# Query products in high and low parts, rotation on VectorE, and one product for the decay rows

## The chip, the cores and the metric

One core of a Trainium2 chip runs the whole kernel in one launch. The engines that matter here: TensorE (PE) multiplies matrices into PSUM banks, VectorE (DVE) and ScalarE (ACT) read those banks and prepare operands, SyncE (SP) issues most transfers, GpSimd (POOL) the rest. Each engine runs its own list of instructions in order and waits on semaphores for the others. The metric is the time of one execution on the device in microseconds (us); lower is better.

## The reference, cut to what matters

The kernel computes one step of a decoder layer for a prompt of 512 tokens and 8 requests of 4 sample tokens (544 columns). The part that is touched is the mixer:

```python
proj = h @ lw['w_in']                      # 44 units of 128 columns
cq = rmsnorm(cq, lw['norm_q_lat'])         # 256 latent features
q = (cq @ lw['w_uq']).reshape(B, T, H_B, NOPE_DIM + ROPE_DIM)
q_rope = rope(q[..., NOPE_DIM:], pos)      # [x1*cos - x2*sin, x2*cos + x1*sin]
kr = rope(kr[:, :, None, :], pos)[:, :, 0, :]
q_lat = jnp.einsum('bthd,chd->bthc', q_nope, lw['w_uk'])
s = jnp.einsum('bthc,bsc->bhts', q_lat, ckv) + jnp.einsum('bthr,bsr->bhts', q_rope, krope)
# softmax of SM_SCALE * s, times ckv, for 8 heads; mLSTM, 4 heads, with decays
D = b[..., :, None] - b[..., None, :] + ic[..., None, :]
```

## The kernel before, in words

Activations lie transposed: 128 features on partitions, tokens as columns. The big products split each fp32 operand in a high part (rounded to the fp32r type) and a low part (the rest), and add three fp32r products: high x high, high x low, low x high. ACT writes the high part (`w_hi`, L1602), DVE the low one (`w_lo`, L2275). One unit of the input projection is 48 such products of 272 columns on PE (L1156). The 41 units from the fourth on are the filler of the whole mixer: on every engine a generator `in_feed` holds its share of the units, and `dense(n)` lets n steps of it pass, a step being one product on PE. What stands between the calls of `dense` is the attention or the mLSTM. The order is thus written out by hand, for each engine by itself.

At the end of each half of a unit DVE evicts it from PSUM (`evict`, L2750). A gate's unit goes to `gt`, ACT writes its tanh to `sg` (`tanh_gate`, L1933), DVE turns that into the gate in `sq` (`gate`, L2765, L2766, L2769), and SP spills `sq` to DRAM (L687). `gt`, `sg` and `sq` have two slots each.

The heads of the attention come in four pairs. For a pair, `query` (L1226) makes three banks of 512 columns, two with the part without rotation (one per head) and one with the rotary part of both heads, each by two fp32 products of `wp` and `cq`; ACT copies them to `qn` and `qrx` (the tile is named accq). `latent_queries` multiplies `qrx` by a permutation matrix (L1233), so that each half of the rotary features stands where the other was, and makes the latent queries (L1235). `rotate` on DVE (L2896 to L2902) multiplies the permuted bank by sin and `qrx` by cos, and adds the two, once in place and twice with the 64-row parts exchanged. `two_scores` (L1257, L1261) waits for it. The keys of the prompt are rotated once in the same way (L1187, L2828 to L2832). The queries of pair 0 stand ahead of the heads; those of pair p+1 stand in the heads of pair p, one bank in each of three places and the latent queries in the fourth.

A head: ACT copies the scores (`take`), DVE masks them and finds the maximum (`highest`), ACT takes exp (`expo`, L2051), DVE divides (`normalise`, L2919), PE transposes (`turn`), ACT copies back (`turned`), PE multiplies by the values. The sample tokens run beside it, through `sample_highest`, `sample_exp`, `sample_turned` (L2082) and `sample_values` (L1329), with the new rows at the start of pairs 0 and 2 (`sample_new`: pnn L2934, prob L2066, L1313).

The mLSTM begins each of its four heads with one fp32 product of 4 rows that spreads the decay row of the head over 128 partitions (L1398); ACT copies it to `nmb`.

## Time and profile before

| | us |
|---|---|
| median of 3 runs | 1341.14 (1340.37 to 1341.49) |
| the profiled execution | 1342.6 |
| its span, first to last instruction | 1340.9 |
| PE busy | 1309.8 (98%) |
| DVE busy | 946.7 (71%) |
| ACT busy | 590.3 (44%) |
| POOL busy | 144.6 (11%) |

The clock that PE was granted is full speed over nearly the whole span (mean 0.998). Busy times of PE overlap, since its products are pipelined: how long one keeps the engine is read from the start of one record to the start of the next, not from its duration. An fp32 product is two records, an fp32r product one. The heads of the attention lie between 478 and 725 us, the mLSTM after that.

### The profile page before, as it was taken

To read this page: it belongs to the slowest core of one execution; us is meant where nothing else is said; L and a number is where in the kernel's file an instruction comes from. 1 tells how busy PE (TensorE), PEld (TensorE's weight loads), DVE (VectorE), ACT (ScalarE), POOL (GpSimd) and SP (SyncE) were. 2 spreads that over 40 slices of the span, in tenths; PEclk is the share of its full clock that TensorE was granted. 3 is DMA by queue.
4 is the path that set the end of the run, shared out by engine and by line. 5 is a ranking of instruction groups with operands and counts; after the bars stand their busy time and mean duration, and the time that the engine had idled before them with its cause. 6 is when DMAs were issued, how large, how long until landed. Compare 5 with 4: busy or idle time off the path is not lost.

```text
span 1340.9 us, 30484 instructions
## 1 busy us (share of the span) xinstructions
PE 1309.8 (98%) x11641; PEld 1229.3 (92%) x11641; DVE 946.7 (71%) x1833; ACT 590.3 (44%) x1127; POOL 144.6 (11%) x275
## 2 busy tenths in 40 slices
PE   9999999999999999999999999999899999999997
PEld 8999999999989968888888888889899999999996
DVE  5999889984497544544444665575889989989556
ACT  5455555652354334433344233233544555555323
POOL 0000000000004105555552000000000000000000
PEclk9999999999999999999999999999999999999999
DMA  4232223322246627777777313414152322233322
GB/s 170 87 124 98 95 95 124 119 88 87 83 183 210 217 79 222 239 217 225 216 226 246 131 64 128 152 48 173 68 184 93 106 95 95 95 106 113 107 87 100
DMA packets 86234, 180.85 MB, mean 135 GB/s; under 512 B 12681, under 2 KB 47498, under 8 KB 84042
## 3 DMA queue, kind: packets, MB, share of 16 engines
q1 hardware_dynamic: 77898, 162.12, 36.1%
q0 software_dynamic: 8192, 16.79, 4.5%
q8 instruction: 93, 1.52, 0.5%
q14 instruction: 51, 0.42, 0.1%
HBM read 162.29 MB, written 16.57 MB: 133 GB/s over the span
## 4 chain that ended last, share of the span: by engine, by line
PE 84%; DVE 8%; DMA 3%; ACT 2%; issue 2%; SPq 0%; DVEq 0%; ACTq 0%
PE acc L1071 20%; PE acc L1156 18%; PE acc L993 12%; PE acc L844 6%; PE bank_a L1071 6%; PE acc L1017 4%; PE acc L905 2%; PE bank_a L1226 2%; PE bank_a L1257 2%; PE acc L1275 1%; PE acc L1297 1%; DMA w_raw<-in_w_gu 1%; PE acc L1329 1%; PE bank_a L1048 1%; PE acc L1301 1%
## 5 line engine op out<-in xcount | busy, mean ns | idle before, releaser
L1071 PE MATMUL acc<-x_forms,pair_w 128*128 128x272 f32 x1728 | 273.2, 289 | 0.0
L1071 PEld LDWEIGHTS acc<-x_forms,pair_w 128*128 128x128 f32 x1728 | 244.4, 188 | 0.0
L1156 PE MATMUL acc<-x_hi,w_hi 128*128 128x272 f32 x656 | 200.2, 305 | 0.0
L1156 PE MATMUL acc<-x_hi,w_lo 128*128 128x272 f32 x656 | 192.2, 293 | 0.0
L1156 PE MATMUL acc<-x_lo,w_hi 128*128 128x272 f32 x656 | 191.9, 292 | 0.0
L2275 DVE TENSOR_TENSOR w_lo<-w_raw,w_hi 128x1024 fp32r<-128x1024 f32 (+1 forms) x92 | 108.3, 1177 | 100.6 <-ACT w_hi L1602 100.3
L482 POOL DMA_DIRECT2D pg<-in_lat x256 | 137.4, 537 | 199.9 <-issue 134.5
L1602 ACT ACTIVATE w_hi<-w_raw 128x1024 fp32r<-128x1024 f32 (+1 forms) x92 | 93.0, 1018 | 90.8 <-PE acc L1156 38.9
L1156 PEld LDWEIGHTS acc<-x_hi,w_hi 128*128 128x128 f32 x656 | 123.8, 189 | 9.6 <-issue 8.1
L1156 PEld LDWEIGHTS acc<-x_lo,w_hi 128*128 128x128 f32 x656 | 123.9, 189 | 5.2 <-issue 4.7
L1156 PEld LDWEIGHTS acc<-x_hi,w_lo 128*128 128x128 f32 x656 | 123.7, 189 | 3.7 <-issue 3.6
L1071 PE MATMUL acc<-x_r,pair_w 128*128 128x272 f32 x384 | 110.7, 288 | 0.0
L2380 DVE TENSOR_TENSOR pair_w<-w_pair,pair_w 128x512 fp32r<-128x512 f32 x128 | 88.3, 690 | 22.8 <-ACT pair_w L1703 19.5
L993 PE MATMUL acc<-h_hi,w_hi 128*128 128x272 f32 x448 | 97.3, 288 | 0.4 <-DVE w_lo L2275 0.4
L993 PE MATMUL acc<-h_hi,w_lo 128*128 128x272 f32 x448 | 96.8, 288 | 0.0
L993 PE MATMUL acc<-h_lo,w_hi 128*128 128x272 f32 x448 | 96.7, 287 | 0.0
L1703 ACT ACTIVATE pair_w<-w_pair 128x512 fp32r<-128x512 f32 x128 | 80.2, 628 | 34.8 <-PE acc L1071 23.2
L1703 ACT ACTIVATE pair_w<-pair_s 128x512 fp32r<-128x512 f32 x96 | 60.3, 632 | 72.6 <-DVE pair_s L2411 32.4
L1071 PE MATMUL bank_a<-x_forms,pair_w 128*128 128x272 f32 x576 | 80.4, 289 | 0.0
L1071 PEld LDWEIGHTS bank_a<-x_forms,pair_w 128*128 128x128 f32 x576 | 75.5, 188 | 0.0
L1071 PEld LDWEIGHTS acc<-x_r,pair_w 128*128 128x128 f32 x384 | 72.4, 189 | 0.0
L993 PEld LDWEIGHTS acc<-h_hi,w_hi 128*128 128x128 f32 x448 | 71.6, 188 | 0.8 <-issue 0.8
(442 smaller groups left out, 2819.6 us busy)
## 6 DMA issues: line engine op xcount, KB each, us to landing
w_pair<-in_w_gu SPq DMA_DIRECT2D x68, 512.0 KB, 4.3
pg<-in_key_t SPq DMA_DIRECT2D x256, 96.0 KB, 2.5
w_raw<-in_w_in SPq DMA_DIRECT2D x44, 512.0 KB, 4.7
pg<-in_lat POOLq DMA_DIRECT2D x256, 64.0 KB, 2.8
w_raw<-in_w_dn SPq DMA_DIRECT2D x32, 448.0 KB, 3.3
w_raw<-in_w_gu SPq DMA_DIRECT2D x20, 512.0 KB, 3.3
block_raw<-in_w_dn SPq DMA_DIRECT2D x32, 256.0 KB, 3.6
g_mid<-sq SPq DMA_DIRECT2D x17, 272.0 KB, 3.0
```

Of the source, the lines that this page charges most:

```text
L482: eng.dma_start(pg[c % 2][:, q, j, PAGE + ROPE:PGW], one(lat, page_of(eng, c, q, j)))\
L844: ins = nc.tensor.matmul(acc[pair][:, a, 0:HT], w[:, slot, n * P:(n + 1) * P], v[:, k, a * HT:(a + 1) * HT], start=first and n == 0 and te ...
L905: ins = nc.tensor.matmul(acc[pair_of[j]][:, a, 0:HT], w, v[:, k, HALF[a]], start=k == 0 and term == 0, stop=k == KD - 1 and term == 2)
L993: ins = nc.tensor.matmul(acc[u // 2 % 2][:, a, 0:HT], w[:, u % 2, n * P:(n + 1) * P], v[:, k, HALF[a]], start=start and n == 0 and term == ...
L1017: ins = nc.tensor.matmul(bank_of[n], w[:, k * P:(k + 1) * P], v[:, k, :], start=start and k == 0 and term == 0, stop=k == KD // 2 - 1 and ...
L1071: ins = nc.tensor.matmul(bank, w[:, k * P:(k + 1) * P], v[:, k, :], start=start and k == 0 and term == 0, stop=k == KD // 2 - 1 and term == 2,
L1156: ins = nc.tensor.matmul(acc[0][:, a, 0:HT], w[:, i % 2, k * P:(k + 1) * P], v[:, k, a * HT:(a + 1) * HT], start=k == 0 and term == 0, sto ...
L1226: ins = nc.tensor.matmul(b[:], wp[:, k * 384 + m * P:k * 384 + (m + 1) * P], cq[:, k, 0:SEQ], start=k == 0, stop=k == 1)
L1602: nc.scalar.activation(whi[:, slot, 0:tiles * P], raw[:, slot, 0:tiles * P], ACT.Copy)\
L1703: nc.scalar.activation(pair_weight_hi(s, n), pair_form(s, n), ACT.Copy).then_inc(pair_hi, 1)
L2275: nc.vector.tensor_tensor(wlo[:, slot, 0:tiles * P], raw[:, slot, 0:tiles * P], f32(whi[:, slot, 0:tiles * P]), ALU.subtract).then_inc(w_s ...
L2380: nc.vector.tensor_tensor(lo, pair_form(s, n), f32(hi), ALU.subtract).then_inc(pair_split, 1)
```

## The change

Four things change.
- The prompt's query products take `cq` and `wp` in high and low parts: six fp32r products for a bank in place of two fp32 ones. ACT makes the high parts, DVE the low ones: of `cq` once, of `wp` for each pair.
- The permutation products of the prompt queries and of the keys are gone. DVE multiplies by sin in pieces of 32 partitions that read one half and write the other (four for the queries, two for the keys), and subtracts instead of adds.
- The decay product reads `rows_hl` and `sel_hl`, of 36 rows: the high parts in rows 0 to 3 and the low parts in rows 32 to 35, zeros between; it is one fp32r product in place of an fp32 one. Both operands are prepared in head 7 of the attention.
- The tanh is written in place, and the gates are made in `gt` and spilled from it; an eviction into a slot of `gt` waits until that slot's last content is staged or spilled (`gate_staged`, `gate_out`). The space of `sg` and `sq` takes the high parts.

```diff
@@ -112,6 +112,10 @@
...
+def in_gt(i):
+    return IN_KIND[i] not in ("q", "k") or i in SPILL_AT
...
@@ -1183,9 +1193,6 @@
...
             pe.wait_ge(d_read, 4)
-            for a in range(2):
-                nc.tensor.matmul(bank_v(f"kr{a}")[0:ROPE, 0:HT], perm[0:ROPE, 0:ROPE],
-                                 kraw[0:ROPE, a * HT:(a + 1) * HT], start=True, stop=True).then_inc(v_ready, 1)
...
@@ -1220,17 +1227,19 @@
             def query(p, m):
-                pe.wait_ge(pair_landed[0], 16 * (3 + p))
+                pe.wait_ge(wp_split, p + 1)
+                pe.wait_ge(cq_split, 1)
...
                 for k in range(2):
-                    ins = nc.tensor.matmul(b[:], wp[:, k * 384 + m * P:k * 384 + (m + 1) * P], cq[:, k, 0:SEQ],
-                                           start=k == 0, stop=k == 1)
+                    at_ = slice(k * 384 + m * P, k * 384 + (m + 1) * P)
+                    for term, (w, v) in enumerate(((wphi, cqhi), (wphi, cqlo), (wplo, cqhi))):
+                        ins = nc.tensor.matmul(b[:], w[:, at_], v[:, k, 0:SEQ],
+                                               start=k == 0 and term == 0, stop=k == 1 and term == 2)
...
             def latent_queries(p):
                 pe.wait_ge(a_read, A.taken(f"q{p}2"))
-                nc.tensor.matmul(bank_v(f"rot{p}")[:], perm, qrx[:, 0:SEQ], start=True, stop=True).then_inc(v_ready, 1)
...
@@ -1395,7 +1404,8 @@
...
                     pe.wait_ge(head0_landed, 16)
-                nc.tensor.matmul(bank_a(f"bm{h}")[:, 0:SEQ], sel[:, h, :], rows2[0:4, 0:SEQ],
+                pe.wait_ge(hl_split, 1)
+                nc.tensor.matmul(bank_a(f"bm{h}")[:, 0:SEQ], sel_hl[:, h, :], rows_hl[:],
...
@@ -1926,11 +1936,7 @@
             def tanh_gate(i):
                 act.wait_ge(d_read, 2 * i + 2)
-                before = [n for n in TANH_AT if n < i and n % 2 == i % 2]
-                if before:
-                    n = before[-1]
-                    act.wait_ge(gate_staged, STAGED_AT[n + 1 if IN_KIND[n] == "o" else n] + 1)
-                nc.scalar.activation(sg[:, i % 2, :], gt[:, i % 2, :], ACT.Tanh, scale=0.5).then_inc(tanh_done, 1)
+                nc.scalar.activation(gt[:, i % 2, :], gt[:, i % 2, :], ACT.Tanh, scale=0.5).then_inc(tanh_done, 1)
...
@@ -1983,6 +1989,8 @@
...
             nc.scalar.activation(ckvtok[0:NS, NT, :], A.bank("cts")[0:NS, 0:P], ACT.Copy).then_inc(a_read, 1)
+            act.wait_ge(cq_ready, 2)
+            nc.scalar.activation(cqhi[:, :, 0:SEQ], cq[:, :, 0:SEQ], ACT.Copy).then_inc(cq_hi, 1)
...
@@ -2012,6 +2020,15 @@
...
+            def split_pair(p):
...
+                act.wait_ge(pair_landed[0], 16 * (3 + p))
+                if p:
+                    act.wait_ge(a_ready, A.filled(f"q{p - 1}2"))
+                nc.scalar.activation(wphi[:], wp[:, 0:768], ACT.Copy).then_inc(wp_hi, 1)
...
+            split_pair(0)
...
@@ -2107,6 +2124,13 @@
...
                     expo(h, 3)
+                    if h == HB - 1:
+                        act.wait_ge(hl_clear, 1)
+                        nc.scalar.activation(sel_hl[0:4, :, :], sel, ACT.Copy)
+                        nc.scalar.activation(sel_hl[32:36, :, :], sel, ACT.Copy)
+                        nc.scalar.activation(rows_hl[0:4, :], rows2[0:4, 0:SEQ], ACT.Copy).then_inc(hl_high, 1)
+                    if h % 2 == 0 and p + 1 < HB // 2:
+                        split_pair(p + 1)
...
@@ -2726,13 +2750,13 @@
...
                     dve.wait_ge(d_half, i + 1)
-                    before = [n for n in range(4, i) if n % 2 == i % 2 and (n in TANH_AT or turned_here(n))]
-                    if i in SPILL_AT and i not in STAGED_AT:
-                        dve.wait_ge(gate_out[SPILL_AT[i] % 2], 16 * (SPILL_AT[i] // 2))
-                    elif before and (i in TANH_AT or turned_here(i)):
+                    before = [n for n in range(4, i) if n % 2 == i % 2 and in_gt(n)]
+                    if before and in_gt(i):
                         n = before[-1]
-                        if n in TANH_AT:
-                            dve.wait_ge(tanh_done, TANH_AT[n] + 1)
+                        if n in SPILL_AT:
+                            dve.wait_ge(gate_out[SPILL_AT[n] % 2], 16 * (SPILL_AT[n] // 2 + 1))
+                        elif n in TANH_AT:
+                            dve.wait_ge(gate_staged, STAGED_AT[n + 1 if IN_KIND[n] == "o" else n] + 1)
...
@@ -2744,29 +2768,24 @@
...
                 out = (ckvraw[:, h_] if kind == "ckv" else cq[:, int(kind[2]), h_] if kind in ("cq0", "cq1") else
-                       sq[:, SPILL_AT[i] % 2, h_] if i in SPILL_AT and i not in STAGED_AT else
-                       qk[:, head % 2, 0, h_] if kind == "q" else qk[:, head % 2, 1, h_] if kind == "k" else
-                       gt[:, i % 2, h_])
+                       gt[:, i % 2, h_] if in_gt(i) else qk[:, head % 2, 0 if kind == "q" else 1, h_])
...
             def gate(i):
...
                 if i in SPILL_AT:
-                    g = SPILL_AT[i]
-                    if g >= 2:
-                        dve.wait_ge(gate_out[g % 2], 16 * (g // 2))
-                    out = sq[:, g % 2, :]
+                    out = gt[:, i % 2, :]
...
@@ -2822,14 +2841,12 @@
...
             dve.wait_ge(c_landed, 32)
-            for a in range(2):
-                h_ = slice(a * HT, (a + 1) * HT)
-                dve.wait_ge(v_ready, V.filled(f"kr{a}"))
-                nc.vector.tensor_tensor(tmp[0:ROPE, h_], V.bank(f"kr{a}")[0:ROPE, 0:HT], sin[0:ROPE, h_], ALU.mult)\
-                    .then_inc(v_read, 1)
-                link(nc.vector.tensor_tensor(krT[0:ROPE, h_], kraw[0:ROPE, h_], cos[0:ROPE, h_], ALU.mult))
-                dve.wait_ge(v_read, V.taken(f"kr{a}"))
-                nc.vector.tensor_tensor(krT[0:ROPE, h_], krT[0:ROPE, h_], tmp[0:ROPE, h_], ALU.add).then_inc(kr_half, 1)
+            dve.wait_ge(d_read, 4)
+            for b in range(2):
+                mine, other = slice(b * ROPE // 2, (b + 1) * ROPE // 2), slice((1 - b) * ROPE // 2, (2 - b) * ROPE // 2)
+                nc.vector.tensor_tensor(tmp[other, :], kraw[mine, :], sin[mine, :], ALU.mult)
+            link(nc.vector.tensor_tensor(krT[0:ROPE, :], kraw[0:ROPE, :], cos[0:ROPE, :], ALU.mult))
+            nc.vector.tensor_tensor(krT[0:ROPE, :], krT[0:ROPE, :], tmp[0:ROPE, :], ALU.subtract).then_inc(kr_half, 2)
...
@@ -2883,23 +2900,35 @@
...
                                     ALU.subtract).then_inc(row_sums, 1)
+            dve.wait_ge(cq_hi, 1)
+            dve.wait_ge(a_ready, A.filled(f"qs{HB // 2 - 1}"))
+            nc.vector.tensor_tensor(cqlo[:, :, 0:SEQ], cq[:, :, 0:SEQ], f32(cqhi[:, :, 0:SEQ]), ALU.subtract)\
+                .then_inc(cq_split, 1)
...
+            def split_pair(p):
...
+                dve.wait_ge(wp_hi, p + 1)
+                nc.vector.tensor_tensor(wplo[:], wp[:, 0:768], f32(wphi[:]), ALU.subtract).then_inc(wp_split, 1)
...
+            split_pair(0)
...
             def rotate(p):
-                dve.wait_ge(v_ready, V.filled(f"rot{p}"))
-                nc.vector.tensor_tensor(tmp[:, 0:SEQ], V.bank(f"rot{p}")[:], sin[:, 0:SEQ], ALU.mult).then_inc(v_read, 1)
+                dve.wait_ge(a_read, A.taken(f"q{p}2"))
+                for b in range(4):
+                    mine, other = slice(32 * b, 32 * b + 32), slice(32 * (b ^ 1), 32 * (b ^ 1) + 32)
+                    nc.vector.tensor_tensor(tmp[other, 0:SEQ], qrx[mine, 0:SEQ], sin[mine, 0:SEQ], ALU.mult)
                 link(nc.vector.tensor_tensor(qr[:, 0:SEQ], qrx[:, 0:SEQ], cos[:, 0:SEQ], ALU.mult))
-                dve.wait_ge(v_read, V.taken(f"rot{p}"))
                 low, high = slice(0, ROPE), slice(ROPE, P)
-                nc.vector.tensor_tensor(qr_turned[high, :], qr[low, 0:SEQ], tmp[low, 0:SEQ], ALU.add)
-                link(nc.vector.tensor_tensor(qr_turned[low, :], qr[high, 0:SEQ], tmp[high, 0:SEQ], ALU.add))
-                nc.vector.tensor_tensor(qr[:, 0:SEQ], qr[:, 0:SEQ], tmp[:, 0:SEQ], ALU.add).then_inc(qr_ready, 1)
+                nc.vector.tensor_tensor(qr_turned[high, :], qr[low, 0:SEQ], tmp[low, 0:SEQ], ALU.subtract)
+                link(nc.vector.tensor_tensor(qr_turned[low, :], qr[high, 0:SEQ], tmp[high, 0:SEQ], ALU.subtract))
+                nc.vector.tensor_tensor(qr[:, 0:SEQ], qr[:, 0:SEQ], tmp[:, 0:SEQ], ALU.subtract).then_inc(qr_ready, 1)
...
@@ -2990,10 +3019,16 @@
...
                     sample_highest(m0)
+                    if h == HB - 1:
+                        dve.wait_ge(a_ready, A.filled(f"q{HB // 2 - 1}2"))
+                        nc.vector.memset(f32(rows_hl[:]), 0.0)
+                        nc.vector.memset(f32(sel_hl[:]), 0.0).then_inc(hl_clear, 1)
...
                     normalise(h, 1)
+                    if h % 2 == 0 and p + 1 < HB // 2:
+                        split_pair(p + 1)
...
@@ -3002,6 +3037,10 @@
...
                     take_output(h)
+                    if h == HB - 1:
+                        dve.wait_ge(hl_high, 1)
+                        nc.vector.tensor_tensor(rows_hl[32:36, :], rows2[0:4, 0:SEQ], f32(rows_hl[0:4, :]), ALU.subtract)\
+                            .then_inc(hl_split, 1)
```

On DVE, the end of head 1 and the rotation of pair 1, before. The name rt is the tile of `qr`, accq that of `qrx`, acc the PSUM bank with the permuted rows:

```order
L2924 COPY olat<-acc 128x512 [waits v_ready]
L2750 TENSOR_TENSOR gt<-acc,rpre 128x272 [waits w_used]
L2275 TENSOR_TENSOR w_lo<-w_raw,w_hi 128x1024 [waits w_hi]
L2896 TENSOR_TENSOR tmp<-acc,consts 128x512 [waits v_ready]
L2897 TENSOR_TENSOR rt<-accq,consts 128x512
L2900 TENSOR_TENSOR qr_turned<-rt,tmp 64x512 [waits v_read,vchain]
L2901 TENSOR_TENSOR qr_turned<-rt,tmp 64x512
L2902 TENSOR_TENSOR rt<-rt,tmp 128x512 [waits vchain]
L2765 TENSOR_SCALAR sg<-sg 128x544 [waits gate_out1,tanh_done]
```

The same place in the changed kernel:

```order
L2953 COPY olat<-acc 128x512 [waits v_ready]
L2772 TENSOR_TENSOR gt<-acc,rpre 128x272 [waits w_used]
L2299 TENSOR_TENSOR w_lo<-w_raw,w_hi 128x1024 [waits w_hi]
L2926 TENSOR_TENSOR tmp<-accq,consts 32x512 [waits a_read]
L2926 TENSOR_TENSOR tmp<-accq,consts 32x512 x3
L2927 TENSOR_TENSOR rt<-accq,consts 128x512
L2929 TENSOR_TENSOR qr_turned<-rt,tmp 64x512 [waits vchain]
L2930 TENSOR_TENSOR qr_turned<-rt,tmp 64x512
L2931 TENSOR_TENSOR rt<-rt,tmp 128x512 [waits vchain]
L2784 TENSOR_SCALAR gt<-gt 128x544 [waits tanh_done]
```

One product from PSUM has become four of 32 partitions from SBUF; the wait is now for ACT's read of the query bank instead of PE's product, and the place behind the w_lo split is the same.

On DVE, head 2 around the second normalise (`pr`) and the eviction behind it, before:

```order
L2918 RECIPROCAL sst<-sst 128x1 [waits ex_ready]
L2919 TENSOR_SCALAR pr<-pr,sst 128x256 [waits vchain]
L2750 TENSOR_TENSOR gt<-acc,rpre 128x272 [waits tanh_done,d_half]
L2918 RECIPROCAL sst<-sst 128x1 [waits ex_ready]
L2919 TENSOR_SCALAR pr<-pr,sst 128x384 [waits vchain]
```

The same place now:

```order
L2947 RECIPROCAL sst<-sst 128x1 [waits ex_ready]
L2948 TENSOR_SCALAR pr<-pr,sst 128x256 [waits vchain]
L2916 TENSOR_TENSOR wp_lo<-wp,wp_hi 128x768 [waits wp_hi]
L2772 TENSOR_TENSOR gt<-acc,rpre 128x272 [waits gate_staged,d_half]
L2947 RECIPROCAL sst<-sst 128x1 [waits ex_ready]
```

The low half of `wp` stands between them and waits for ACT. On ACT, in the changed kernel, the last exp of head 2 is followed by:

```order
L2068 ACTIVATE pr,sst<-pr,sst 128x384 [waits mx_ready]
L2068 ACTIVATE pr,sst<-pr,sst 128x512 [waits mx_ready]
L2029 ACTIVATE wp_hi<-wp 128x768 [waits a_ready,pair_landed0]
L2099 ACTIVATE probT<-acc 128x512 [waits o_ready,turn_ready]
```

Before, the copy to probT followed the exp at once. PE's list of this head now waits for wp_split ahead of the query products.

## Rows read from the trace of the kernel before

**Rows 1.** The page, busy time, share of the span and instructions of an engine.
```profile
PE 1309.8 (98%) x11641; PEld 1229.3 (92%) x11641; DVE 946.7 (71%) x1833; ACT 590.3 (44%) x1127; POOL 144.6 (11%) x275
```

**Rows 2.** Busy time by stretches, the attention stretch: us, then each engine's busy us.
```profile
478.00:725.00 247.00, 245.18 (x3347) 201.21 (x3345) 122.22 (x325) 101.44 (x244) 120.39 (x228) 1.00 0.70 209
```

**Rows 3.** Waits of PE, 395 to 880 us: total us, times, longest.
```profile
PE acc L1418 <- DVE pt L3034: 1.5, 4, 0.4
...
```

**Rows 4.** Timeline of PE: start us, us, engine, line, operation, tiles, shapes, count.
```profile
468.84 0.29 PE L1156 MATMUL acc<-x_lo,w_hi 128*128 128x272 f32 x1
...
469.97 0.29 PE L1156 MATMUL acc<-x_lo,w_hi 128*128 128x272 f32 x1
...
472.48 5.31 PE L1226 MATMUL bank_a<-cq,wp 128*128 128x512 f32 x12
...
725.14 1.12 PE L1398 MATMUL bank_a<-rpost,consts 4*128 4x512 f32 x2
726.11 0.30 PE L1401 MATMUL bank_a<-rpost,consts 4*128 4x32 f32 x2
```

**Rows 5.** Timeline, rotation of pair 0 (bracketed: idle before, what ended it).
```profile
479.40 1.23 DVE L2275 TENSOR_TENSOR w_lo<-w_raw,w_hi 128x1024 fp32r<-128x1024 f32 x1 [6.28 <-ACT w_hi L1602]
...
480.54 0.69 DVE L2896 TENSOR_TENSOR tmp<-acc,consts 128x512 f32<-128x512 f32 x1
...
483.89 0.18 DVE L2934 TENSOR_TENSOR pnn<-acc,consts 128x32 f32<-128x32 f32 x1
...
484.99 0.28 PE L1313 MATMUL acc<-consts,prob 128*32 128x128 f32 x1 [0.94 <-ACT prob L2066]
```

**Rows 6.** Timeline, rotation of pair 1 and the scores that follow on PE.
```profile
543.57 0.68 DVE L2896 TENSOR_TENSOR tmp<-acc,consts 128x512 f32<-128x512 f32 x1
544.17 0.68 DVE L2897 TENSOR_TENSOR rt<-accq,consts 128x512 f32<-128x512 f32 x1
...
544.88 0.69 DVE L2900 TENSOR_TENSOR qr_turned<-rt,tmp 64x512 f32<-64x512 f32 x1
545.58 0.69 DVE L2901 TENSOR_TENSOR qr_turned<-rt,tmp 64x512 f32<-64x512 f32 x1
546.31 0.69 DVE L2902 TENSOR_TENSOR rt<-rt,tmp 128x512 f32<-128x512 f32 x1
...
547.39 0.92 PE L1257 MATMUL bank_a<-ckvT,ql 128*128 128x128 f32 x4
```

**Rows 7.** Timeline, before the rotations of pairs 2 and 3 and after them.
```profile
600.31 0.43 DVE L2750 TENSOR_TENSOR gt<-acc,rpre 128x272 f32<-128x272 f32 x1
...
606.57 0.35 DVE L2959 SCALAR_TENSOR_TENSOR o_acc<-o_acc,sm_al,acc 128x128 f32<-128x128 f32 x1 [0.81 <-PE acc L1329]
...
664.43 0.43 DVE L2750 TENSOR_TENSOR sq<-acc,rpre 128x272 f32<-128x272 f32 x1
...
671.46 0.71 PE L1257 MATMUL bank_a<-ckvT,ql 128*128 128x128 f32 x3
```

**Rows 8.** Timeline, head 2: second normalise, last exp, next query on PE.
```profile
555.35 0.35 DVE L2919 TENSOR_SCALAR pr<-pr,sst 128x256 f32<-128x256 f32 x1
...
555.91 0.19 ACT L2051 ACTIVATION_READ_ACCUMULATOR pr<-pr,sst 128x1 f32 x1
...
557.66 1.88 PE L1226 MATMUL bank_a<-cq,wp 128*128 128x512 f32 x4
```

**Rows 9.** Timeline, head 7: the copy to probT and the products that read it.
```profile
707.68 0.58 ACT L2082 ACTIVATE probT<-acc 128x512 f32<-128x512 f32 x1
...
709.60 1.08 PE L1329 MATMUL acc<-pg,probT 128*32 128x128 f32 x32
```

**Rows 10.** The page's DMA issues (count, KB, us to landing); two timeline rows.
```profile
g_mid<-sq SPq DMA_DIRECT2D x17, 272.0 KB, 3.0
...
465.90 0.35 SPq L687 DMA_DIRECT2D g_mid<-sq  x1
...
469.68 0.44 DVE L2750 TENSOR_TENSOR gt<-acc,rpre 128x272 f32<-128x272 f32 x1 [0.81 <-PE acc L1156]
```

More of the change, by code:

```diff
@@ L199, in layer @@
         sq = put("sq", [P, 2, T])
+        wphi, cqhi = at("wp_hi", [P, 768], SG_AT, F32R), at("cq_hi", [P, 2, T], SQ_AT, F32R)
         w_pair0 = at("w_pair0", [P, 2, 2 * QW], SQ_AT)
@@ L248, in layer @@
         probT = put("probT", [P, 2, SEQ])
+        CQ_AT = cursor[0]
+        cqlo = at("cq_lo", [P, 2, T], cursor[0], F32R)
         cq = put("cq", [P, 2, T])
+        wplo = at("wp_lo", [P, 768], cursor[0], F32R)
         wp = put("wp", [P, 1024])
@@ L300, in layer @@
         wuv = put("wuv", [P, HB * P])
+        assert cursor[0] <= CQ_AT
+        cursor[0] = CQ_AT
+        rows_hl = put("rows_hl", [36, SEQ], F32R)
+        sel_hl = put("sel_hl", [36, HA, P], F32R)
         gl1 = put("gl1", [P, 2, 2, T])
@@ L325, in layer @@
         A.plan(["lat0", "lat1", "latq0", "latq1", "ct", "cts"])
-        V.plan(["kr0", "kr1"])
         for p in range(HB // 2):
@@ L333, in layer @@
                 A.plan(["q00", "q01", "q02", "ql00", "ql01"])
-                V.plan(["rot0"])
             for h in (2 * p, 2 * p + 1):
@@ L340, in layer @@
                 V.plan([f"o{h}"])
-                if h % 2 and p + 1 < HB // 2:
-                    V.plan([f"rot{p + 1}"])
         for h in range(HA):
@@ L377, in layer @@
         head0_landed = sem("head0_landed")
+        hl_clear, hl_high, hl_split = sem("hl_clear"), sem("hl_high"), sem("hl_split")
+        cq_hi, cq_split, wp_hi, wp_split = sem("cq_hi"), sem("cq_split"), sem("wp_hi"), sem("wp_split")
         vt_ready, vt_read = sem("vt_ready"), sem("vt_read")
@@ L686, in in_feed @@
                                 sp.wait_ge(d_read, 2 * i)
-                            sp.dma_start(g_mid[g], sq[:, g % 2, :]).then_inc(gate_out[g % 2], 16)
+                            sp.dma_start(g_mid[g], gt[:, (i - 1) % 2, :]).then_inc(gate_out[g % 2], 16)
                         yield
@@ L2764, in gate @@
                 if IN_KIND[i] == "ga":
-                    link(nc.vector.tensor_scalar(sg[:, 0, :], sg[:, 0, :], 0.25, 0.25, ALU.mult, ALU.add))
-                    nc.vector.scalar_tensor_tensor(out=out, in0=sg[:, 1, :], scalar=1.0, in1=sg[:, 0, :],
+                    link(nc.vector.tensor_scalar(gt[:, 0, :], gt[:, 0, :], 0.25, 0.25, ALU.mult, ALU.add))
+                    nc.vector.scalar_tensor_tensor(out=out, in0=gt[:, 1, :], scalar=1.0, in1=gt[:, 0, :],
                                                    op0=ALU.add, op1=ALU.mult).then_inc(gate_staged, 1)
                 else:
-                    nc.vector.tensor_scalar(out, sg[:, i % 2, :], 0.5, 0.5, ALU.mult, ALU.add)\
+                    nc.vector.tensor_scalar(out, gt[:, i % 2, :], 0.5, 0.5, ALU.mult, ALU.add)\
                         .then_inc(gate_staged, 1)
```

## The prediction

> **What bounds the kernel now.** I read the busy shares first: TensorE (PE) is busy 98% of the span [rows 1]. Then the table by stretches: between 478 and 725 us, the attention stretch in which nearly all of the change lies, PE has work for 245.2 of 247.0 us, while VectorE (DVE) is busy half of the time [rows 2]. Then the waits of PE over 395 to 880 us: six groups, the largest 1.5 us in sum [rows 3]. So each product that is removed is worth its own time, as long as the engines that feed PE keep up. Whether they do can't be read from busy shares, so I went through the timeline at every place where the change puts work on DVE or ScalarE (ACT), and compared when PE needs the result.
>
> **What PE loses and gains.** A 128x512 fp32 product stands as two records. The 12 records of three queries run from 472.48 at 0.429 us each, 0.86 us a product [rows 4]. Dense fp32r records of 272 columns follow one another by 0.126 us: ten in a row, the first at 468.84 and the last at 469.97 [rows 4]. For 512 columns the trace has no fp32r record. Scaled by columns it is 0.235; at half an fp32 record it is 0.215. I take the middle, 0.225.
> - Queries: 12 queries of 2 fp32 products become 12 of 6 fp32r products: 1.72 against 1.35, so 0.37 each and 4.4 us together (3.7 to 5.1 by the two ends).
> - The four prompt rotations: 4 x 0.86 = 3.4 us.
> - The key rotation: four records of 272 columns at 0.429 x 272/512 = 0.23: 0.9 us.
> - Decay rows: 725.14 to 726.11 is 0.97 us for one product of 4 rows [rows 4]; one fp32r product is 0.225, so 0.74 each and 3.0 us for four heads. That the new one has 36 rows I price at nothing; the fp32 rows with 4 rows are dearer, not cheaper, than those with 128. The copy to nmb and everything behind it starts as much earlier as PE does, so this gain holds.
> Sum on PE: 11.7 us.
>
> **What DVE takes in return.** The rotation had five DVE instructions. The first starts at 543.57, the last at 546.31 and ends at 547.00 [rows 6]: 3.43 us. Now it has eight: four products of 32 partitions that write into other partitions, and the four others. An instruction on 32 partitions has the same 512 columns. The nearest rows are the two pieces of 64 partitions that also move across partitions: 0.70 from start to start (544.88 to 545.58), 0.69 long [rows 6]. Four such (2.80), then the cosine product (0.70), the two turned pieces (0.70, 0.73) and the last (0.69) as before: 5.62 us, 2.2 more. The cheap end is the pitch of two instructions on all partitions, 543.57 to 544.17, 0.60 [rows 6]: 5.22 us, 1.8 more. The dear end I take from the 128x1024 split, 1.23 [rows 5]: were each shifted product as long as that, 7.74 us.
>
> The Trainium skill ("VectorE: DVE Perf Modes", section "Two Vector instructions with no wait between them") says that a Vector instruction which begins in another group of 32 partitions than the one before it, in what it reads or writes, starts only when the earlier ones have finished. The trace agrees: 0.70 where the partitions change, 0.60 where they don't [rows 6]. By that rule the four new intervals cost 0.70 each; without it they would cost 0.60, and with three of the four pairs on the path the gain would be 1.2 us larger, 4.8 in place of 3.6.
>
> Does it show on PE? Pair by pair:
> - Pair 0: the rotation starts at 480.54, behind the split w_lo (479.40), which waits for ACT's w_hi [rows 5]; ACT makes that behind its copies of the three queries. These end 1.10 us earlier now. The last rotation instruction is followed by pnn at 483.89, and PE waits for that chain already: L1313 starts at 484.99 after 0.94 us idle [rows 5]. The rotation's extra 2.2 us less 1.1 puts pnn and L1313 1.1 later than before. So the 1.10 of the queries and the 0.86 of the rotation are lost here, and 1.1 more: 3.06 lost.
> - Pair 1: the rotation starts at 543.57 behind a w_lo split that hangs on the end of a unit on PE. It ended at 547.00 and the scores followed at 547.39 [rows 6], with 0.4 to spare. Now it ends 2.2 later, at 549.2, scores at about 549.35: 1.95 later than before instead of 0.86 earlier, 2.8 lost.
> - Pair 2: DVE waited here for the PE product. It can start behind the eviction at 600.31 [rows 7], at 600.74, and ends at 606.36. The scores have room, but the sample accumulation (606.57 before, [rows 7]) and the chain behind it, which PE meets without slack, move only 0.17 earlier: 0.7 lost.
> - Pair 3: start 664.87 behind the eviction at 664.43, end 670.5; the scores would be at 671.46 - 0.86 = 670.6 [rows 7]. 0.1 lost.
>
> **The halves of w_pair.** For each of pairs 1 to 3, ACT writes the high half behind its last exp of the even head, DVE the low half behind the second normalise. At 555.70 DVE is done, at 556.10 ACT's accumulator read, and PE starts the next query at 557.66 [rows 8], 13 dense products later. High half: ACT's copy of 512 columns took 0.58 [rows 9], so 768 take 0.58 to 0.87; I take 0.82, since part of the 0.58 doesn't grow. Low half: 768/1024 of 1.23, 0.92 [rows 5]. From 556.1 that is 557.84, and about 0.1 for the two handovers. 0.27 lost, three times: 0.8. If ACT and DVE are 0.3 faster this is nothing, at most 1.5 in all. Behind it on DVE stand an eviction and two normalises, on ACT the turned copies; PE asks for those over 3 us later, so they are free. The split of cq and of pair 0, and the longer key rotation, stand where DVE and ACT idle (DVE waited 6.28 us before its w_lo at 479.40, [rows 5]).
>
> **Head 7.** ACT gets three copies of 4x512 at 0.58, 1.75 us, ahead of a weight split, a tanh and the copy to probT that ended at 708.26; PE uses it at 709.60 [rows 9]. Room 1.3, so 0.45 to 0.5 lost, and 0.1 for the two memsets on DVE. The last subtraction is done long before the first decay product.
>
> **Gates in place.** Evictions of units now wait for the spill of the unit two before. A spill lands after 3.0 us (median of 17) [rows 10]. The tightest is issued at 465.90 and the next eviction into that slot is at 469.68 [rows 10]: 0.8 to spare at the median, and PE asks for that eviction only at the next unit. I price it at nothing; a landing 3 us later would still be hidden there.
>
> **Sum.** Lost: 3.06 + 2.8 + 0.7 + 0.1 + 0.8 + 0.6 = 8.1. Net 11.7 - 8.1 = 3.6 us faster. The profiled execution took 1342.6 (span 1340.9 and 1.7 around it), so 1339.0 for it; the median of the runs is 1341.14, 1.5 lower, and I forecast 1341.14 - 3.6 = 1337.5.
>
> **Rivals.**
> 1. DVE's longer rotation is hidden: another engine's start, not DVE's, sets the scores. Then all 11.7 come through but 0.8 and 0.6: 10.3 faster, 1330.8. For it: in pairs 2 and 3 DVE waited for the PE product, which is gone. Against: pair 0, where PE is seen waiting, and the 0.4 us of pair 1.
> 2. Slower: the shifted products are dear. The place is the four rotations; each 0.1 us more on a product is 0.4 us on a rotation, 1.6 us in all, since pairs 0 to 3 are by then all on the path. At 0.93 us a product (0.70 + 0.225) the gain is gone; at 1.23 it is 8.5 us dearer: 4.9 slower, 1346.0. For it: no row shows a 32-partition shifted product. Against: 64 and 128 partitions take the same 0.69.
> 3. No change to tell: fp32r at 512 columns is at the dear end (4.4 becomes 3.7, decay 2.9), the splits cost 1.5 and head 7 1.0: 0.7 + 0.1 + 0.7 + 0.4 = 1.9 less, so 1.7 faster, 1339.4.
> That the change doesn't do what it says I rule out: in the order of PE the rotation products are gone and the query products are fp32r.
>
> **Chances.** Forecast (2.7 to 5.5 faster) 0.52; rival 1 and what lies on the way to it 0.15; rival 3 and other mixes within 2.7 us 0.25; rival 2 and anything else that is slower 0.08. A difference under 0.2% (2.7 us) can't be told from none. Faster by more: 0.52 + 0.15 = 0.67; within: 0.25; slower: 0.08. The range: from the cheap ends (pitch 0.60, fp32r 0.215, splits free: 3.6 + 1.2 + 0.9 + 0.8 = 6.5, and part of the way to rival 1), 1333.5, to just under no gain, 1341.0.
>
> **What would show it.** In the changed profile: fp32r query records at 0.22 to 0.235; shifted products 0.69 long at 0.70; PE waiting about 2 to 3 us for the rotation at pair 1 and for prob at pair 0, under 0.3 at pair 3; short waits of 0.3 for the low half at heads 0, 2 and 4; the decay product about 0.74 shorter, four times. If PE shows no wait for DVE at pairs 0 and 1, rival 1 holds; if shifted products are over 0.9 long, rival 2. I am wrong as well if evictions wait for spills long enough to hold PE.

## The result, and the profile after

The changed kernel took 1344.95 us (median of 12 runs, 1342.14 to 1348.42) against 1341.54 us for the kernel before (12 runs, 1340.30 to 1344.74). The ratio is 1.0024, 95% interval 1.0017 to 1.0032: 3.4 us slower, where 3.6 us faster was forecast, and outside the range. Twelve further runs of it, in a later comparison, gave 1.0027 (1.0018 to 1.0037); of the 23 runs of the kernel before beside them, one took 2123.3 us at a mean clock of 0.555 and is in no ratio. The profiled execution took 1343.75 us, with a span of 1342.1 and a mean granted clock of 0.994, where the kernel before had 0.998.

The page of the changed kernel, busy shares (against [rows 1]) and the TensorE clock in 40 slices:

```profile
PE 1304.8 (97%) x11649; PEld 1233.8 (92%) x11649; DVE 961.7 (72%) x1851; ACT 596.2 (44%) x1135; POOL 145.1 (11%) x275
PEclk9999999999999989999999999999999999999999
```

PE has 8 records more, as the edits have it: 24 more for the queries, 12 fewer for the rotations of queries and keys, 4 fewer for the decay rows. Its busy time fell by only 5.0 us, in part since some records became longer (0.43 us for a dense one at 485 us, below, against 0.29 in [rows 4]). One slice of the clock reads 8, where the kernel before has forty nines. The two largest waits of PE over 395 to 900 us, against [rows 3] (to 880 us), where the largest sum was 1.5 us:

```profile
PE acc L1322 <- ACT prob L2083: 4.1, 1, 4.1
PE bank_a L1266 <- issue: 2.8, 1, 2.8
```

L1322 is the first sample turn, at pair 0; L1266 the first scores of pair 1 ("issue" names no releaser; it stands behind DVE's rotation). Their places in the timeline, DVE and PE, against [rows 5, 6]:

```profile
476.61 1.23 DVE L2299 TENSOR_TENSOR w_lo<-w_raw,w_hi 128x1024 fp32r<-128x1024 f32 x1 [5.31 <-ACT w_hi L1612]
477.87 2.77 DVE L2926 TENSOR_TENSOR tmp<-accq,consts 32x512 f32<-32x512 f32 x4
480.66 0.69 DVE L2927 TENSOR_TENSOR rt<-accq,consts 128x512 f32<-128x512 f32 x1
...
483.41 0.18 DVE L2963 TENSOR_TENSOR pnn<-acc,consts 128x32 f32<-128x32 f32 x1
...
484.51 0.40 PE L1322 MATMUL acc<-consts,prob 128*32 128x128 f32 x1 [4.12 <-ACT prob L2083]
...
485.16 0.43 PE L1166 MATMUL acc<-x_hi,w_lo 128*128 128x272 f32 x1
485.39 0.43 PE L1166 MATMUL acc<-x_hi,w_hi 128*128 128x272 f32 x1
...
545.31 2.77 DVE L2926 TENSOR_TENSOR tmp<-accq,consts 32x512 f32<-32x512 f32 x4
...
550.25 0.69 DVE L2931 TENSOR_TENSOR rt<-rt,tmp 128x512 f32<-128x512 f32 x1
...
551.04 0.89 PE L1266 MATMUL bank_a<-ckvT,ql 128*128 128x128 f32 x4 [2.81 <-issue]
```

The eight rotation instructions take 477.87 to 483.41, 5.54 us, and the four shifted ones stand 0.70 apart (480.66 less 477.87, over four): as priced. Both waits, too, came out as worked out. What the prediction had no term for is in the two dense rows at 485: 0.23 us from start to start, where dense products stand 0.126 apart [rows 4]. Busy time by stretches (after POOL's: granted clock, DMA share, GB/s), against [rows 2], says why:

```profile
478.00:484.00 6.00, 2.40 (x32) 1.98 (x30) 5.79 (x12) 0.31 (x1) 0.00 (x0) 0.99 0.29 90
484.00:488.00 4.00, 3.49 (x39) 2.97 (x43) 1.81 (x5) 0.69 (x3) 0.00 (x0) 0.50 0.18 70
488.00:492.00 4.00, 4.00 (x77) 2.83 (x72) 0.58 (x2) 0.60 (x2) 0.00 (x0) 0.66 0.00 0
...
550.00:555.00 5.00, 3.96 (x57) 2.86 (x58) 4.13 (x13) 1.76 (x6) 3.15 (x6) 0.72 0.83 230
```

At each of the two waits TensorE is then granted half of its clock, 1.2 GHz in place of 2.4: in the clock records from 483.92, 0.6 us before the first wait ends, for 6.83 us, and from 552.19, 1.2 us behind the second, for 3.41 us. The kernel before has no such stretch between its first instructions and 1334 us. The Trainium skill ("TensorE: Matmul & The Clock Gate", section "What's actually happening") describes this: half rate is the engine's resting state and only activity lifts it. The rows agree as far as they go: in the 6 us ahead of the first fall DVE is busy for 5.79 and PE for 2.40, and full clock is back at 490.75, 6.2 us after PE went on with its work.

### The profile page after: what moved, and what is told of

Same layout as the page of the kernel before. It is cut to its first block, busy times and chain, and to the rows that moved or that the text cites. A ratio compares the mean times of both kernels' runs of the same rounds, so it can differ in the third digit from the quotient of the medians.

```text
span 1342.1 us, 30492 instructions
## 1 busy us (share of the span) xinstructions
PE 1304.8 (97%) x11649; PEld 1233.8 (92%) x11649; DVE 961.7 (72%) x1851; ACT 596.2 (44%) x1135; POOL 145.1 (11%) x275
## 4 chain that ended last, share of the span: by engine, by line
PE 82%; DVE 9%; DMA 3%; issue 3%; ACT 3%; SPq 0%; DVEq 0%; ACTq 0%
PE acc L1081 20%; PE acc L1166 16%; PE acc L1003 12%; PE acc L854 6%; PE bank_a L1081 6%; PE acc L1027 4%; PE acc L915 2%; PE bank_a L1266 2%; PE acc L1284 1%; PE bank_a L1236 1%; PE acc L1306 1%; DVE w_lo L2299 1%; PE acc L1338 1%; PE acc L1310 1%; DMA w_raw<-in_w_gu 1%
```

## The experiments

Theory T, written down before the runs: the longer rotation on DVE makes PE wait at pairs 0 and 1, and each of these waits is followed by a stretch at half clock; waits and clock together turn a gain of about 8 us into a loss. R1: the waits count, the clock falls for another reason. R2: the loss comes from the rest of the change. Each ratio is to the kernel before on the same chip.

**Rotation back on TensorE** (`e1`).

```diff
-                dve.wait_ge(a_read, A.taken(f"q{p}2"))
-                for b in range(4): ...
+                dve.wait_ge(v_ready, V.filled(f"rot{p}"))   # five instructions and the PE product, as before
```

> The changed kernel with the rotation of the prompt queries given back to TensorE (permutation product, five VectorE instructions); key rotation, queries by fp32r, decay rows and gates in place stay. Theory T (the longer rotation on VectorE makes PE wait at pairs 0 and 1, and each wait is followed by a stretch at half of the granted clock): no half-clock stretch between 478 and 725 us, mean clock 0.998, PE idle before the first sample turn back near 1 us, time 1341.5 - (1.15 key rotation + 3.8 queries + 1.8 decay rows) + 0.9 splits + 0.5 head 7 = about 1336.5. Rival R1 (the waits count but the clock falls for another reason, so it falls here too): mean clock 0.994 to 0.995, about 1340.5 to 1341. Rival R2 (the loss comes from the rest of the change: splits, gates in place, spills): no faster than the changed kernel, since PE has 3.4 us more to do: 1345 to 1348.

1337.84 us, ratio 0.9961 (0.9947 to 0.9975): 5.2 us faster than before by the ratio. The clock was 0.996 in four runs of five and 0.998 in one, with 1335.76. R2 falls: the rest of the change is there and the kernel is faster than before. No stretch at half clock stands at 484 or 552, but its trace has one at 558.59, and a wait that nobody had named:

```profile
535.45 14.28 SPq L484 DMA_DIRECT2D pg<-in_key_t  x16
...
550.26 0.42 SPq L769 DMA_DIRECT2D wp<-in_w_pair  x1
...
556.75 0.84 ACT L2033 ACTIVATE wp_hi<-wp 128x768 fp32r<-128x768 f32 x1 [2.33 <-DMA wp<-in_w_pair]
557.62 0.96 DVE L2920 TENSOR_TENSOR wp_lo<-wp,wp_hi 128x768 fp32r<-128x768 f32 x1 [3.60 <-ACT wp_hi L2033]
558.64 0.79 PE L1239 MATMUL bank_a<-cq_hi,wp_hi 128*128 128x512 f32 x1 [2.50 <-DVE wp_lo L2920]
```

Once the first two waits are gone, the next pair's weights land too late for the halves: SP issues their load (550.26) behind sixteen key page loads, it lands 6.5 us later, and the high half could have begun at 554.4 but for it (556.75 less 2.33). The query itself would have been asked for at 556.1 (558.64 less 2.50), so as two fp32 products it would have waited some 0.6 us. In the changed kernel the load is issued at 551.55 and ACT begins the high half at 561.18 without a wait for it: what was lost at pairs 0 and 1 hid this.

**Rotation on VectorE alone**, in the kernel before (`e2`): the reverse of that diff.

> The kernel before with one edit: the prompt queries are rotated on VectorE by four shifted products, and the permutation products are gone. Theory T: PE idle before the first sample turn about 3 us, before the scores of pair 1 about 2 us, each followed by several us at half clock; lost by waits about 2.2 + 1.5 at pairs 0 and 1 net of the 0.86 saved, 0.9 gained at pairs 2 and 3, and about 4 us by the clock: 1341.5 + 3 + 4 = about 1348, mean clock 0.994 to 0.995. R1: the waits but no fall of the clock: about 1344.5, clock 0.998. R2: the rotation costs nothing to speak of: 1338 to 1341.5.

1349.32 us, ratio 1.0051 (1.0037 to 1.0064), clock 0.991 to 0.994. The two largest waits of PE:

```profile
PE acc L1309 <- ACT prob L2062: 4.1, 1, 4.1
PE bank_a L1253 <- issue: 2.8, 1, 2.8
```

The same two waits to the tenth, and half clock for 6.83 us from 484.95 and again from 553.22. The waits are longer than expected (3 and 2 us), the time is near (1348). This one edit brings the whole loss; it costs 6.8 us although it takes 3.4 us of products off PE.

**The waits filled** (`e3`): VectorE's work unchanged, PE kept at work; the extra products' results are overwritten unread.

```diff
+            def fill_in(name, n):   # 30 ahead of sample_turn(0), 20 ahead of two_scores(2, 0)
+                b = bank_v(name)
+                for _ in range(n):
+                    nc.tensor.matmul(b[:, 0:HT], wphi[:, 0:P], cqhi[:, 0, 0:HT], start=True, stop=True)
```

> The changed kernel with fp32r products of 272 columns, whose results are overwritten unread, put on PE ahead of the two waits: 30 ahead of the first sample turn (wait 4.1 us, filled for 3.8) and 20 ahead of the scores of pair 1 (wait 2.8 us, filled for 2.5). VectorE's work and its times stay. Theory T: the two waits end at the same times as before (turn about 484.5, scores about 551), but no half-clock stretch follows: mean clock 0.997 to 0.998, 4.4 us faster than the changed kernel, about 1340.5. R1 (clock falls for another reason, or its fall doesn't cost): clock stays 0.994, time 1345 or up to 1 us more. R2: the same as R1.

1339.40 us, ratio 0.9981 (0.9972 to 0.9990), clock 0.996 to 0.998. The timeline and the stretches of this kernel:

```profile
481.63 3.96 PE L1260 MATMUL acc<-cq_hi,wp_hi 128*128 128x272 f32 x30
485.90 0.28 PE L1332 MATMUL acc<-consts,prob 128*32 128x128 f32 x1 [0.31 <-ACT prob L2093]
486.15 0.29 PE L1166 MATMUL acc<-x_lo,w_hi 128*128 128x272 f32 x1
486.28 0.29 PE L1166 MATMUL acc<-x_hi,w_lo 128*128 128x272 f32 x1
```
```profile
478.00:484.00 6.00, 6.00 (x56) 5.28 (x55) 5.86 (x8) 1.61 (x3) 0.00 (x0) 1.00 0.27 90
484.00:488.00 4.00, 3.69 (x58) 3.19 (x60) 3.11 (x9) 0.68 (x3) 0.00 (x0) 1.00 0.16 64
```

Useful work begins again no earlier than in the changed kernel: 485.90 against 484.51, 1.39 later, by as much as this execution was late already at its first query product (472.06 against 470.67). And yet the kernel is 5.8 us faster (0.9981 against 1.0024, intervals apart; 4.2 to 7.4 by the two intervals), by nothing but products whose result nobody reads. The dense rows are back at 0.13, and between 16 and 1333 us the clock doesn't fall. This parts wait and clock: R1 falls, and the clock's share is the larger part of the miss. The 4.4 us that were expected lie within what the intervals allow. In the two profiled executions the way from the first sample turn to the eviction after the next scores, and from the scores of pair 1 to the eviction behind them, is 18.74 and 14.07 us in the changed kernel, 15.98 and 12.83 in the filled one, so 2.8 + 1.2 = 4.0; but that execution of the changed kernel had clock 0.994 and 1343.75 us, and its other runs went down to 0.991, with 1348.42.

```profile
503.25 0.44 DVE L2772 TENSOR_TENSOR gt<-acc,rpre 128x272 f32<-128x272 f32 x1 [0.54 <-PE acc L1166]
...
565.11 0.44 DVE L2772 TENSOR_TENSOR gt<-acc,rpre 128x272 f32<-128x272 f32 x1 [0.64 <-PE acc L1166]
```
```profile
501.88 0.44 DVE L2782 TENSOR_TENSOR gt<-acc,rpre 128x272 f32<-128x272 f32 x1 [0.53 <-PE acc L1166]
...
562.90 0.44 DVE L2782 TENSOR_TENSOR gt<-acc,rpre 128x272 f32<-128x272 f32 x1 [0.67 <-PE acc L1166]
```

(The first fence is the changed kernel, the second the filled one, whose scores of pair 1 start at 550.07. Counted from the eviction ahead of them, at 541.53 here and 542.90 there, that is 8.5 us against 8.1: the extra products put them 0.4 us late, and 3.6 of the 4.0 is what the fill gained in these two executions.)

**Both rotations early** (`e4`): the same VectorE instructions where VectorE stood idle.

```diff
+            rotate(0)            # four products and the cosine product only
+            sample_highest(0)    # was in sample_new
             dense(6)
-            rotate(0)
+            rotate_sums()        # the other three
             dense(6)
...
                     dense(26)
+                    if h % 2 and p + 1 < HB // 2:
+                        rotate(p + 1)
                     sample_sum(m0)
                     sample_highest(m1)
                     dense(18)
+                    if h % 2 and p + 1 < HB // 2:
+                        rotate_sums()
                     take_output(h)
...
-                    if h % 2 and p + 1 < HB // 2:
-                        rotate(p + 1)
```

> The changed kernel with the same VectorE instructions in another place: for pair 0 the four shifted products and the cosine product ahead of the weight split and the sample maximum ahead of that, the three sums behind; for pairs 1 to 3 the products ahead of the odd head's first sample accumulation and the sums ahead of the take of the values, where VectorE stood idle (531.3 to 536.6 and 539.0 to 541.4 us). Theory T: both waits under 1 us, no half-clock stretch, mean clock 0.998; all gains come through: 1341.5 - (1.15 + 3.8 + 3.4 + 1.8) + 0.9 + 0.5 + 0.5 left idle at pair 0 = about 1333.7, faster than both kernels. R1 (clock falls all the same): about 1338. R2: over 1340.

1334.83 us, ratio 0.9943 (0.9929 to 0.9956). DVE at pair 0 in this kernel:

```profile
474.81 2.77 DVE L2926 TENSOR_TENSOR tmp<-accq,consts 32x512 f32<-32x512 f32 x4 [4.36 <-ACT accq L2040]
477.60 0.69 DVE L2927 TENSOR_TENSOR rt<-accq,consts 128x512 f32<-128x512 f32 x1
478.33 0.19 DVE L2966 TENSOR_TENSOR pnn<-acc,consts 128x32 f32<-128x32 f32 x1
```
```profile
484.00:488.00 4.00, 4.00 (x59) 2.13 (x52) 2.64 (x12) 1.92 (x7) 0.00 (x0) 1.00 0.31 104
```

(The last line is the stretch behind it: PE busy throughout, full clock.) The maximum chain runs at 478.33 in place of 483.41, PE no longer waits for it, the largest wait at pair 0 is 0.4 us, and the clock doesn't fall before the kernel's end. Nothing was taken off any engine: the gain was there and was lost to the places of four rotations of 5.5 us on VectorE. The 7.6 us by the ratio are near the 7.8 expected.

**One place at a time** (`e5`, `e6`): the first half of that diff alone, then the second alone.

> The changed kernel with the early place for the rotation of pair 0 only; pairs 1 to 3 stay as changed. Theory T: no half-clock stretch at 484, the one after the scores of pair 1 stays; mean clock about 0.996; against the version with both moved (7.2 us under before) it loses pair 1's wait and clock (3.56 + 0.86) and 0.7 at pair 2: about 5.1, so 2 to 2.5 us under before, ratio 0.9982 to 0.9985. Rival (one place carries nearly all): ratio 0.9945 if pair 0 is that place, 1.002 if pair 1 is.

> The changed kernel with the early place for the rotations of pairs 1 to 3 only; pair 0 stays as changed. Theory T: PE idle 4.1 us before the first sample turn and 6.8 us at half clock behind it, nothing at pair 1; mean clock 0.995 to 0.996; against the version with both moved it loses about 5.5 us, so 1.5 to 2 us under before, ratio 0.9985 to 0.999. Rival (one place carries nearly all): ratio 0.9945 if pair 1 is that place, 1.002 if pair 0 is.

Ratio 0.9972 (0.9962 to 0.9983) and 1.0002 (0.9993 to 1.0011). Between 16 us and the kernel's end the profiled runs have half clock only where a rotation is late: from 547.96 for 3.41 us with pair 0 early, from 484.55 for 3.41 us with the others early. Neither place carries all. Against 0.9943, leaving pairs 1 to 3 late costs 3.9 us and leaving pair 0 late 7.9; 5.1 and 5.5 were expected. The sum, 11.8, is near to the 11.3 by which 1.0027 and 0.9943 differ. The clock at pair 0 varies: the profiled run of the version with pair 0 late, its fastest (1339.51), fell for 3.41 us only, while its other ten runs had clocks down to 0.994 and took up to 1343.40. That version's trace also has 1.38 us of wait for the low half, behind a late load of the weights as in `e1`, where `e4` has 0.65.

**Sizes: decay rows, queries** (`e7`, `e8`). The changed kernel with the old decay product `sel[:, h, :], rows2[0:4, 0:SEQ]`, then with the old `query` on `wp` and `cq`.

> The changed kernel with the mLSTM decay rows by the fp32 product of 4 rows as before, and without the clears, copies and subtraction of head 7. As the trace of the changed kernel has it (0.44 us a head, 0.5 at head 7): 1.76 - 0.5 = 1.3 us slower than the changed kernel, ratio to before about 1.0034. As the prediction had it (0.74 a head, 0.6): 2.4 us slower, ratio 1.0042. Rival (the decay rows gain nothing): ratio 1.002 or less.

> The changed kernel with the twelve prompt queries by two fp32 products each, straight from w_pair and c_q, and none of the halves. As the trace of the changed kernel has it (0.32 us a query, 0.3 lost at heads 0, 2 and 4): 3.8 - 0.9 = 2.9 us slower than the changed kernel, ratio to before about 1.0046. Rival (the queries by halves gain nothing, as the waits for halves eat it): ratio 1.0024 or less.

1345.60 us, 1.0027 (1.0018 to 1.0036), and 1345.95 us, 1.0029 (1.0014 to 1.0044). Both intervals hold the changed kernel's 1.0024, so by the times alone neither size is shown, and the rivals are not ruled out. The traces tell more. From an eviction at 403 to 405 us to one behind the attention and three decay rows the changed kernel needs 446.84 us and the version with old queries 449.65, 2.8 more, with the same two stretches at half clock in both; 2.9 was expected. (First fence changed, second old queries.)

```profile
403.70 0.79 DVE L2772 TENSOR_TENSOR ckvraw<-acc,rpre 128x272 f32<-128x272 f32 x2 [0.42 <-ACT rpre L1690]
...
850.54 0.43 DVE L2772 TENSOR_TENSOR gt<-acc,rpre 128x272 f32<-128x272 f32 x1
```
```profile
403.08 0.79 DVE L2764 TENSOR_TENSOR ckvraw<-acc,rpre 128x272 f32<-128x272 f32 x2 [0.42 <-ACT rpre L1687]
...
852.73 0.43 DVE L2764 TENSOR_TENSOR gt<-acc,rpre 128x272 f32<-128x272 f32 x1
```

For the decay rows, PE in the changed kernel, then with the old product:

```profile
728.49 0.50 PE L1408 MATMUL bank_a<-rows_hl,sel_hl 36*128 36x512 f32 x1
728.92 0.40 PE L1411 MATMUL bank_a<-rpost,consts 4*128 4x32 f32 x2
729.16 0.39 PE L1412 MATMUL bank_a<-sml,consts 4*128 4x40 f32 x2
```
```profile
728.40 1.12 PE L1407 MATMUL bank_a<-rpost,consts 4*128 4x512 f32 x2
729.36 0.30 PE L1410 MATMUL bank_a<-rpost,consts 4*128 4x32 f32 x2
729.50 0.39 PE L1411 MATMUL bank_a<-sml,consts 4*128 4x40 f32 x2
```

0.43 + 0.24 = 0.67 us in place of 0.96 + 0.14 = 1.10: 0.43 saved a head, not 0.74. The single fp32r product takes 0.43, not 0.225, to the start of the next, and the fp32 product of 32 columns behind it 0.10 more than behind fp32. Whether the 36 rows or the change between the two forms of product brings this was not tried.

**Half of the fill** (`e9`): 15 products in place of 30, 8 in place of 20.

> The filled version with fewer products: 15 in place of 30 ahead of the first sample turn, 8 in place of 20 ahead of the scores of pair 1, so PE still idles about 2.2 and 1.8 us there; the waits end at the same times. If any wait of this length is enough for the clock to fall: mean clock 0.994 to 0.995, half-clock stretches at 484 and 552, time as the changed kernel, ratio to before about 1.002. If it takes a wait nearer to the 2.5 to 4.1 us that were followed by a fall so far (waits of 0.9 and 1.3 us were not): clock 0.997, ratio 0.998 as with the full fill. A fall behind one of the two only, ratio between.

1340.82 us, ratio 0.9997 (0.9986 to 1.0009), between the two. PE waited 2.2 and 1.6 us. In the profiled run the clock fell behind the first (3.41 us from 486.12), not behind the second; the twelve runs spread from 0.993 (1345.60) to 0.997 (1339.93). That is the third outcome that was written down, a fall behind one of the two only. The spread of the mean clocks suggests that a wait of this length is followed by a fall in some executions and by none in others; with one trace of this version that is not shown here, but see the list at the end.

**Tuned** (`e10`): `e4` with three more moves.

```diff
+                                if q == 3 and c % 4 == 3 and p + 2 < HB // 2:
+                                    load_pair(p + 2)          # SP, inside the key page loads
                                 key_pages(sp, c + 2, q)
...
+                    if h % 2 == 0 and p + 1 < HB // 2:        # ACT, was behind expo(h, 3)
+                        split_pair(p + 1)
                     expo(h, 3)
+                    if h == HB - 2: ...                       # the two copies of sel (and their clears on DVE), was HB - 1
```

> The version with both rotations early and three more moves: the load of the next pair's weights is issued ahead of the last four of sixteen key page loads in place of behind them (its landing held ACT's high half for 0.48 us at head 2), ACT writes the high half ahead of its last exp of the even head, and the two copies of the selector for the decay rows stand at head 6, with only the copy of the rows at head 7. If the 0.3 us waits at heads 0, 2 and 4, the late landing and the 0.5 us at head 7 are what is left: 0.8 + 0.4 + 0.5 = 1.7 us faster than the version with both rotations early, ratio to before about 0.993. If those waits are replaced by others (the later exp, the page load behind): no faster, ratio 0.9943.

1333.28 us, ratio 0.9935 (0.9921 to 0.9948): the expected size, though its interval overlaps with that of `e4`, so against that the gain is not shown by the times. It beats both kernels, the one before by 8.7 us. Its trace has no wait of PE for the low half left, and the changed kernel beside it (`e11`) fell as before:

> The changed kernel once more, beside the versions of this call on one chip: mean clock 0.993 to 0.995, ratio 1.002 to 1.003 as in its first runs; the two half-clock stretches again behind the waits at 480 and 548 us.

1345.09 us, ratio 1.0027 (1.0018 to 1.0037), clock 0.991 to 0.994; half clock for 6.83 us from 483.27 and for 3.41 us from 551.53, at the same two places.

## Why the prediction was wrong

**The step that failed** is "Does it show on PE? Pair by pair". It priced what PE loses at a wait as the length of the wait. The lengths were right: at pair 0 L1322 was to move so that PE idles 4.0 us (0.94 + 3.06), and it idled 4.1, though the list of signs said 2 to 3 for it; at pair 1 2.8 was forecast and 2.8 came. But no term stood for the rate at which PE works behind a wait. By the filled version that is about 5.8 us in the median run, 4.0 in the profiled ones; the forecast of 3.6 faster less 4.0 is already a loss.

The same evictions in the two kernels show where it went. Before:

```profile
472.68 0.44 DVE L2750 TENSOR_TENSOR gt<-acc,rpre 128x272 f32<-128x272 f32 x1 [2.56 <-PE acc L1156]
...
500.98 0.44 DVE L2750 TENSOR_TENSOR gt<-acc,rpre 128x272 f32<-128x272 f32 x1 [1.76 <-PE acc L1156]
...
541.28 0.44 DVE L2750 TENSOR_TENSOR gt<-acc,rpre 128x272 f32<-128x272 f32 x1 [0.82 <-PE acc L1156]
...
559.95 0.44 DVE L2750 TENSOR_TENSOR gt<-acc,rpre 128x272 f32<-128x272 f32 x1 [2.77 <-PE acc L1156]
```

In the changed kernel the first and the third stand so (the second, 503.25, and the fourth, 565.11, are shown above):

```profile
470.87 0.44 DVE L2772 TENSOR_TENSOR gt<-acc,rpre 128x272 f32<-128x272 f32 x1 [2.57 <-PE acc L1166]
...
542.90 0.44 DVE L2772 TENSOR_TENSOR gt<-acc,rpre 128x272 f32<-128x272 f32 x1 [0.82 <-PE acc L1166]
```

Around pair 0 the way grew from 28.30 to 32.38 us, by 4.1 where 1.1 was worked out; around pair 1 from 18.67 to 22.21, by 3.5 where 1.95 was. That is 4.6 more than forecast, and the clock has 4.0 of it.

The trace of the kernel before had a warning, at its end, which was not read for this: PE's last products start at 1330.67, and from 1334.66 on the clock is half.

```profile
1330.00:1335.00 5.00, 1.33 (x8) 0.71 (x6) 4.36 (x11) 1.44 (x4) 0.00 (x0) 0.97 0.65 217
1335.00:1340.90 5.90, 0.00 (x0) 0.00 (x0) 3.09 (x7) 0.00 (x0) 0.00 (x0) 0.50 0.54 189
```

**Terms that were mis-sized.** Decay rows: 0.74 a head forecast, 0.43 measured, 1.2 us in all. Queries: 0.37 forecast, 0.32 measured, 0.6 us in all; an fp32r record of 512 columns stands 0.232 us before the next (six, from 470.67 to 472.06, 1.39), near the dear end of what was bounded, by columns. Together with the clock: 5.8 + 1.2 + 0.6 = 7.6, against a miss of 7.0. The first term is known to no better than 1.6 us, so that the sum fits is not a proof of each.

```profile
470.67 0.39 PE L1236 MATMUL bank_a<-cq_hi,wp_hi 128*128 128x512 f32 x1
...
472.06 0.40 PE L1236 MATMUL bank_a<-cq_hi,wp_hi 128*128 128x512 f32 x1
```

**Terms that held.** The rotation's 5.62 us (5.54). The key rotation: 0.9 forecast, 1.07 by the evictions ahead of it and behind (419.59 and 435.47 before, 418.67 and 433.48 now). Pair 2: 0.7 lost of 0.86, so 0.16 gained, was forecast, 0.14 came (600.31 to 607.95 before, 604.84 to 612.34 now). Pair 3: 0.76 gained was forecast, 0.87 came (654.35 to 689.44 before, 658.04 to 692.26 now). The low half: at head 2 the query starts at 563.05, 0.33 behind the dense product ahead of it, where dense products stand 0.126 apart, so 0.2 of wait (0.27 forecast); head 4 has the same. Head 7: PE waits 0.40 us for the copy to probT, where 0.45 to 0.5 was forecast. PE's waits show none for an eviction that waits for a spill.

```profile
712.93 1.08 PE L1338 MATMUL acc<-pg,probT 128*32 128x128 f32 x32 [0.40 <-ACT probT L2099]
```

**The rivals.** Rival 2 ended on the right side, at 1346.0, for a wrong reason: the shifted products cost what was forecast, not more. Rival 1, the rotation hidden, does not hold in this order of the program; `e4` shows that 7.6 of its 10.3 us were there for a better place, and `e10` 8.7. It is the waits' second price that no case contained; slower had 0.08, too small a chance.

**A tight place that stayed hidden.** The weights' load was taken to be there in time. In the changed kernel it is, with the time lost at pairs 0 and 1 ahead of it; in `e1` PE waits 2.5 us for what hangs on it, in `e6` 1.4, in `e4` 0.65. So of the gain that the forecast counted ahead of it a part would not have come through.

## What to carry to other kernels

Where an engine that sets the time is made to wait, price two things: the length of the wait, and the rate at which the engine starts again. For TensorE look in the trace for any place where it stands idle for microseconds, at the start and the end too, and read the granted clock behind it. When work moves to an engine with free time, ask where in its order the work lands: four rotations of 5.5 us on VectorE cost some 11 us more at one set of places than at another, though each engine has the same work.

## What the hardware showed unexpectedly

- How often the clock fell at a wait of TensorE, over the thirteen profiled executions, from 395 us to the end of PE's work: at a wait of 4.1 us in six of six, at one of 2.8 us in six of six, at 2.5 and at 2.2 us in the one case each; at 1.8 (twice), 1.6 and 1.4 us and below never.
- All thirteen have one more wait, before 12 us, ahead of all that differs between them (for x_lo on VectorE). It varies by itself: at 2.56, 2.36, 2.32, 2.21 and 2.08 us a fall of 3.41 us followed, at 2.12 none, at 1.83 one, at the six others, 1.91 us and less, none. So near 2 us it is decided by something that these traces don't show, and every comparison of single runs has up to 1.7 us of noise in it by this (an estimate: half of 3.41).
- The falls at the 4.1 us wait lasted 6.83 us in the four traces where they began 0.6 to 1.4 us before the wait ended, and 3.41 us in the two where they began 0.4 and 0.6 us behind it. Of the falls at 2.8 us five lasted 3.41 us and one 6.83. What decides this was not tried.
- Products whose results nobody reads made a kernel 5.8 us faster (1.0024 to 0.9981).
